# A hybrid decoder layer on one core: the mixer's queues rearranged

## The reference, cut to what matters

```
proj = xn @ w_in                      # one projection, 51 column tiles of 128
A: three groups (window, dilation) = (128,1), (512,4), (2048,16), 4 heads of 64:
   o_g = softmax(q k^T, banded) v ;  lse_g
   alpha = softmax over the groups of lse ;  o_a = sum_g alpha_g * o_g
B: gated delta rule, 4 heads of 128: conv + silu on q, k, v; L2 norms of q, k; chunks;
   per chunk (I + M) u = rhs, M strictly lower triangular; state carried on
   o_b = rms_norm(o_b) * silu(z)
y = sigmoid(gate_a) * (o_a @ w_pa) + sigmoid(gate_b) * (o_b @ w_pb) ;  out = y @ w_o
```

## Time and profile before

| | |
|---|---|
| three runs, median (range) | 1662.61 us (1659.88 to 1666.7) |
| the profiled execution | 1656.37 us |
| its span | 1654.6 us |
| mean granted clock of TensorE | 0.978 |
| PE, PEld busy | 94%, 77% |
| DVE, ACT, POOL busy | 59%, 41%, 52% |

### The profile page before, as it was taken

One profiled execution on the slowest core, in us unless ns is written; L12 is line 12 of the kernel. 1 busy time (PEld: TensorE's weight loads), 2 busy tenths in 40 slices (PEclk: granted clock), 3 DMA queues, 4 the chain that ended last, 5 costly groups with the idle time before them and its releaser, 6 DMA issues.

```text
span 1654.6 us, 21066 instructions
## 1 busy us (share of the span) xinstructions
PE 1554.6 (94%) x7625; PEld 1280.4 (77%) x7625; DVE 971.3 (59%) x1421; ACT 676.6 (41%) x1059; POOL 863.1 (52%) x675
## 2 busy tenths in 40 slices
PE   6998878989999998789999999999999999999998
PEld 4787657878888787668778877788888888888886
DVE  6743424556464657565355136865655666688876
ACT  5754322223434353443432133544444444454445
POOL 4567655655545443335733346988887778200011
PEclk9999989999999999899999999999999999999999
DMA  5132433334354444333437121333333333697685
GB/s 168 58 102 77 121 88 104 101 113 134 111 163 112 127 137 125 111 86 100 150 117 278 54 102 45 96 98 112 96 102 102 102 102 105 215 324 227 191 265 181
DMA packets 228147, 215.26 MB, mean 130 GB/s; under 512 B 25764, under 2 KB 176844, under 8 KB 228044
## 3 DMA queue, kind: packets, MB, share of 16 engines
q1 hardware_dynamic: 227824, 213.83, 41.9%
q10 hardware_dynamic: 220, 0.09, 0.0%
HBM read 156.85 MB, written 57.02 MB: 129 GB/s over the span
## 4 chain that ended last, share of the span: by engine, by line
PE 74%; DVE 10%; POOL 4%; DMA 4%; SPq 3%; ACT 3%; issue 2%; DVEq 0%; ACTq 0%; POOLq 0%
PE acc L1796 17%; PE acc L2852 12%; PE acc L2862 7%; PE bank_ab L2852 7%; PE att_ps L2852 5%; PE acc L672 5%; PE bank_ab L1745 5%; PE bank_ab L2862 3%; PE att_ps L2862 3%; PE acc L2221 3%; DMA m<-m_d 2%; DVE prod L1517 1%; PE bank_ab L2221 1%; PE att_ps L2221 1%; PE att_ps L1862 1%
## 5 line engine op out<-in xcount | busy, mean ns | idle before, releaser
L1241 POOL TENSOR_TENSOR w_low<-w_raw,w_high 128x512 fp32r<-128x512 f32 x96 | 126.1, 1314 | 173.0 <-ACT w_high L1335 172.7
L1796 PE MATMUL acc<-xh,w_high 128*128 128x512 f32 x384 | 160.4, 418 | 12.4 <-ACT m_one L1346 9.7
L1796 PE MATMUL acc<-xl,w_high 128*128 128x512 f32 x384 | 152.9, 398 | 0.0
L1796 PE MATMUL acc<-xh,w_low 128*128 128x512 f32 x384 | 152.7, 398 | 0.0
L1241 POOL TENSOR_TENSOR w_low<-m_sum,w_high 128x512 fp32r<-128x512 f32 x72 | 98.2, 1364 | 97.8 <-ACT w_high L1335 97.8
L1796 PE MATMUL acc<-m_t_high,w_high 128*128 128x512 f32 x288 | 120.5, 418 | 13.4 <-POOL w_low L1241 13.3
L1796 PE MATMUL acc<-m_t_high,w_low 128*128 128x512 f32 x288 | 114.7, 398 | 0.0
L1796 PE MATMUL acc<-m_t_low,w_high 128*128 128x512 f32 x288 | 114.5, 397 | 0.0
L2628 POOL TENSOR_TENSOR f_h<-f_h,f_fw 128x512 f32<-128x512 f32 x8 | 11.3, 1416 | 171.2 <-ACT f_junk L2551 171.2
L1796 PEld LDWEIGHTS acc<-xh,w_high 128*128 128x128 f32 x384 | 74.5, 194 | 28.5 <-issue 11.6
L1796 PEld LDWEIGHTS acc<-xh,w_low 128*128 128x128 f32 x384 | 73.8, 192 | 16.7
(11 more groups left out here) (438 smaller groups left out, 4540.2 us busy)
## 6 DMA issues: line engine op xcount, KB each, us to landing
w_raw<-in_w_in_dram SPq DMA_DIRECT2D x96, 256.0 KB, 3.3
f_raw<-glu_d SPq DMA_DIRECT2D x66, 256.0 KB, 3.1
f_raw<-in_w_down_dram SPq DMA_DIRECT2D x55, 256.0 KB, 4.2
w_raw<-in_w_up_dram SPq DMA_DIRECT2D x24, 512.0 KB, 5.2
glu_d<-u_free_high SPq DMA_DIRECT2D x22, 512.0 KB, 4.7
u_raw_even<-in_w_up_dram SPq DMA_DIRECT2D x20, 512.0 KB, 4.9
att_d<-staging SPq DMA_DIRECT2D x18, 512.0 KB, 3.4
f_raw<-gsum_d SPq DMA_DIRECT2D x33, 256.0 KB, 3.6
```

The costliest lines, as they stand in the source:

```text
L1241: g.tensor_tensor(vl[n % RING], source[it[2]], vh[n % RING].bitcast(F32), ALU.subtract).then_inc(s_vlo, 1)
L1796: mm = t_.matmul(to, w[:, k, :], xx[:, k, :], start=i < 4 and k == 0 and j == 0, stop=k == HK - 1 and j == 2, skip_group_check=True)
```

## The change

Eight edits, all in the order or the place of mixer work:

- `rnorm` becomes four items at (5,2), (5,3), (6,2), (6,3), each a power of 128x16; the tiny products of VectorE move to `rowsT`.
- `silu`, `gatesum` and `ssq` of the first convolution job move to later steps; the first split moves a step earlier.
- The delta rule starts 5 steps later (`DN_FROM`); its first solution stands further behind `kkD`; `T4` follows `P4` at once.
- The solution has four pieces: `sv0` for rows 2 to 4, `sv1` for rows 5 to 7, `sv2` and `sv3` for the two block products. `ts` moves behind the last.
- A new item `xb`: the product `XB` (L1638) goes from VectorE to GpSimd.
- The merging's three products and two sums go from VectorE to GpSimd; VectorE keeps the weights.
- For tiles 0 to 5 the two transposes of the merged tile stand in `a_pv` of the unit two later, in the other bank; their copy is ScalarE's there. For tiles 6 and 7 `cmbT` stays, later, with its copy on VectorE.
- The staged gates are stored raw (Copy); the sigmoid is taken in the merging stage, one activation a feature tile. The load of the row factors of the next chunk moves behind `ml`.

```diff
-        return [[(name, c)] for name in ("ml", "sv0", "sv1", "sv2", "ts", "tl", "ex")]
+        return [[(name, c)] for name in ("ml", "sv0", "sv1", "sv2", "sv3", "ts", "tl", "ex")]
...
+    out = [("load", 0)] + rest * 3 + [("xb", 0)] + kt + rest + kkD + rest * 3 + ml + rest * 2 + sv0 + rest + sv1 + rest
+    out += sv2 + rest + sv3 + rest
...
+        out += xb + [("vq", c)] + kt + [("P4", c), ("T4", c)] + kkD + rest + [("P5", c)] + ml + [("T5", c)] + ob + sv0
+        out += [("P6", c)] + sv1 + [("kS", c), ("T6", c)] + sv2 + [("vn", c)] + sv3 + ts + [("so", c)] + tl + ex
...
+RN = ((5, 2), (5, 3), (6, 2), (6, 3))
+CMB_LAST = {NT - 2: 20, NT - 1: 22}
-DN_FROM = 5 * TURN + 2 * HK
+DN_FROM = 5 * TURN + 3 * HK + 1
...
+                    part = rr[:].rearrange("p a h c -> p (a h c)")[:, j * n:(j + 1) * n]
+                    g.tensor_tensor(part, part, hp64[:, 0:n], ALU.pow).then_inc(s_rr, 1)
...
+                if kind == "cmb":
+                    i = it[1]
+                    X, cbs = cb, cbs2[i % 2]
+                    oc = ocb[:].rearrange("p (h c) -> p h c", h=AH)
+                    pool.wait_ge(s_co, 2 * i + 1)
+                    for q in range(NG):
+                        step(g.tensor_tensor(X[:, q, :, 0:DH], X[:, q, :, 0:DH],
+                                             cbs[:, 3, q].unsqueeze(2).to_broadcast([P, AH, DH]), ALU.mult))
+                    if i:
+                        pool.wait_ge(s_oast, 16 * i)
+                    step(g.tensor_tensor(oc, X[:, 0, :, 0:DH], X[:, 1, :, 0:DH], ALU.add))
+                    g.tensor_tensor(oc, oc, X[:, 2, :, 0:DH], ALU.add).then_inc(s_co, 1)
...
+                    if name == "xb":
+                        pool.wait_ge(s_rl, 16 * (c + 2))
+                        pool.wait_ge(s_ckqk[c % 2], 16 * (c // 2 + 1))
+                        if c:
+                            pool.wait_ge(s_a, a_taken[("kkD", c - 1)])
+                        g.tensor_tensor(XB[:], ckqk[c % 2][:, NH:2 * NH, :], spread[:, 1], ALU.mult).then_inc(s_dtm, 1)
...
-                            g.activation(stg[:], a[:], ACT.Sigmoid).then_inc(s_taken, 1)
+                            g.activation(stg[:], a[:], ACT.Copy).then_inc(s_taken, 1)
...
+                    act.wait_ge(s_atpe, att_no[it])
+                    if kind == "a_pv" and it[1] in merged_at:
+                        g.activation(ocb[:], att1[:, 2 * P:4 * P], ACT.Copy).then_inc(s_vk, 1)
...
+                    if it[1] in merged_at:
+                        pe.wait_ge(s_co, 2 * merged_at[it[1]] + 2)
+                        for j in range(2):
+                            last = t_.transpose(att1[:, (2 + j) * P:(3 + j) * P], ocb[:, j * P:(j + 1) * P], ident[:])
...
+                act.wait_ge(s_gate[(m + 1) % 2], 16 * ((m + 1) // 2))
+                nc.scalar.activation(gates[:, (m + 1) % 2], gates[:, (m + 1) % 2], ACT.Sigmoid).then_inc(s_gact, 1)
```

More of the change, by code:

```diff
@@ L118, in solving @@
     def solving(c):
-        return [[(name, c)] for name in ("ml", "sv0", "sv1", "sv2", "ts", "tl", "ex")]
+        return [[(name, c)] for name in ("ml", "sv0", "sv1", "sv2", "sv3", "ts", "tl", "ex")]
     rest = [("rest", None)]
-    ml, sv0, sv1, sv2, ts, tl, ex = solving(0)
+    ml, sv0, sv1, sv2, sv3, ts, tl, ex = solving(0)
     kt, kkD = front(0)
-    out = [("load", 0)] + rest * 3 + kt + rest + kkD + rest * 2 + ml + rest + sv0 + rest * 3 + sv1 + sv2 + rest
+    out = [("load", 0)] + rest * 3 + [("xb", 0)] + kt + rest + kkD + rest * 3 + ml + rest * 2 + sv0 + rest + sv1 + rest
+    out += sv2 + rest + sv3 + rest
     out += ts + rest + tl + rest * 2 + ex + rest
@@ L154, in mixer_schedule @@
                           1: [("split", 0, 0), ("sum", 0, 3), ("T", "low3")],
-                          2: [("T", "high1"), ("silu", 1)], 3: [("gatesum",), ("T", "low1")],
-                          4: [("split", 0, 1), ("sum", 0, 4)], 6: [("ssq", 0)]}.get(k, [])
+                          2: [("T", "high1")], 3: [("split", 0, 1), ("sum", 0, 4), ("T", "low1")],
+                          5: [("silu", 1)], 6: [("gatesum",)]}.get(k, [])
         items.append(("evac", n))
@@ L182, in mixer_schedule @@
                     items.append(("one", p))
+                    if p == 0:
+                        items.append(("ssq", 0))
                     if p == 0:
@@ L244, in mixer_schedule @@
                             c = u[1]
-                            for d, step in ((3, ("cload", c)), (9, ("cmbA", c)), (12, ("cmb", c)), (17, ("cmbT", c))):
+                            steps = [(3, ("cload", c)), (9, ("cmbA", c)), (12, ("cmb", c))]
+                            steps += [(CMB_LAST[c], ("cmbT", c))] if c in CMB_LAST else []
+                            for d, step in steps:
                                 at_slot.setdefault(slot + d, []).append(step)
@@ L710, in mixer @@
     unit_no = count(units)
+    merged_at = {(0, c + 2): c for c in range(NT) if c not in CMB_LAST}
+    v_done, oc_done, copies = {}, {}, 0
+    for u in units:
+        if u in merged_at:
+            copies += 1
+            oc_done[merged_at[u]] = copies
+        if unit_no[u] < len(units):
+            copies += 1
+            v_done[unit_no[u] + 1] = copies
     stores = [u for u in units for _ in range(2 if u[0] == 2 else 1)]
@@ L718, in mixer @@
         assert c == 0 or order[("cmb", c - 1)] < order[("cload", c)]
-        assert c == 0 or order[("cmbT", c - 1)] < order[("cmb", c)]
+        assert c not in oc_done or order[("cmb", c)] < order[("a_pv", (0, c + 2))] < order[("cmb", c + 1)]
     s_tri, s_const, s_masks, s_small = sem("m_gate_masks_ready"), sem("m_const_step"), sem("m_masks_ready"), sem("m_small_loaded")
@@ L1243, in x_gpsimd @@
                 if kind == "rnorm":
[L1244 to L1250, removed]
@@ L1507, in solve @@
             def solve(part, c):
-                if part == 0:
-                    dve.wait_ge(s_ml, 16 * (c + 1))
-                    if c:
-                        dve.wait_ge(s_ts, 16 * c)
-                    link(g.tensor_copy(strided(t_, BASE, [diag, 2], [1, 1]), strided(m_, 1, [diag, 2], [1, 1])))
-                    for i in range(2, half):
+                if part < 2:
+                    if part == 0:
+                        dve.wait_ge(s_ml, 16 * (c + 1))
+                        if c:
+                            dve.wait_ge(s_ts, 16 * c)
+                        link(g.tensor_copy(strided(t_, BASE, [diag, 2], [1, 1]), strided(m_, 1, [diag, 2], [1, 1])))
+                    for i in (range(2, half - 3), range(half - 3, half))[part]:
                         pr = strided(prod[0:NBLK * NH], 0, [i * i, 2], [i, i], [1, i])
@@ L1522, in solve @@
                 low = strided(t_, half * BASE, [BASE, half], [1, half])
-                if part == 1:
+                if part == 2:
                     link(g.tensor_tensor(pr, strided(m_, half, [1, half], [0, half], [BASE, half]),
```

81 lines of the change are left out of this document (41 added, 40 removed).

## The result

| | before | changed |
|---|---|---|
| median of four runs, one chip | 1661.24 us (1657.45 to 1666.7) | 1619.9 us (1616.26 to 1624.55) |
| ratio, 95% interval | | 0.975 [0.971, 0.979] |
| the profiled execution, its span | 1656.4, 1654.6 us | 1621.0, 1619.2 us |
| mean granted clock of TensorE | 0.978 | 0.992 |

The forecast was 1620 us. Between the profiled executions it promised 42.5 us, and 35.4 came.

A forecast was written before the change was run, and what follows sets the result against it. TensorE, busy 84 to 95% of the mixer, bounds the kernel; only gaps and slow-clock stretches can be won. Terms sum to -42.5 us, from 1656.4 to 1613.9 profiled; adding 6.2 gives a 1620 us median, own range 1602 to 1638.

The forecast's parts named there:

- Opening, -3: Product of squares, which waits 2.4 us for ScalarE, moves three k-steps later: -3 us, bounds -4 and +2.
- Later first loads, -3: Chunks' first loads go behind the weight room GpSimd's sum needs, easing w_low waits: -3 us, bounds -6 and +3.
- Powers in pieces, 0: GpSimd's row-norm power in four pieces: one w_low wait becomes two, about 4.4 and 5.1 us; net 0.
- all covered: Best bound of the powers term, -9.9 us: TensorE's whole wait for w_low there gone.
- First solution, -8.5: First solution 15 steps behind kkD, not 9: TensorE's 9.7 us wait goes, a 3.5 us cost appears; -8.5 us.
- Solution in pieces, -9 and -8: Half a solution's first part moves behind the copies of P6 and O: -9 us for P6, -8 for O.
- Merging, -25: Merging on GpSimd, transposes beside the values' product, raw gates: transposes wait for exponentials alone; -25 us, bounds -32 and -10.
- Spreading, +14: GpSimd waits for the solution's load at the spreading, delaying low parts of weights: +14 us, bounds 0 and +35.
- Sigmoid in the merging stage, 0: Six activations of 1.9 us while ScalarE is otherwise idle there: 0 us, bounds 0 and +6.
- New waits eat half: Rival, chance 0.17: GpSimd's added work passes waits on, spreading at its upper +35; about 1641 us.
- Slower: Rival, chance 0.07: SP issues the solution's load late, GpSimd stands 7 us longer in seven chunks; about 1680 us.
- It doesn't do what it says: Rival, chance 0.05: VectorE and the exponentials were the merging's real limit, not ScalarE's copy; 1655 us.

The follow-up runs named there:

- e1: Changed kernel with the powers of the row norms in one piece of 128x64 in place of four; 1619.5 us, 0.975 of before.
- e3: Changed kernel with the first part of a solution whole again, ahead of the copies of P6 and O; 1629.2 us, 0.982 of before.
- e4: Changed kernel with the first chunk's solution 9 steps behind its kk product again, in two neighbouring parts; 1622.7 us, 0.978 of before.
- e5: Changed kernel with the merging's three products and two sums back on VectorE; 1642.8 us, 0.989 of before.
- e7: Changed kernel with the merged tiles' transposes back in their old place and all their copies on ScalarE; 1627.2 us, 0.980 of before.
- e8: Changed kernel with merging on VectorE, sigmoid at the gates' evacuation, and transposes apart with ScalarE's copy; 1656.1 us, 0.9965 of before.
- e12: e11 with two GpSimd sums of 128x2048 cut into eight of 128x512 and the first chunk's matrix load three k-steps later; 1599.3 us, 0.962 of before.
- e11: Changed kernel with powers as ScalarE square root and VectorE reciprocal, and the spreading moved behind the next item; 1599.0 us, 0.964 of before.

## Why the prediction was right, point by point

*Opening, -3: right, and covered in the profile.* The wait for the product of squares is gone. In `e1` and `e3` the ninth copy starts at 157.5 us, 2.9 before that of the kernel before. In the changed kernel's own profile it starts at 161.9, since a later rise of the clock, and the collision of VectorE with GpSimd at 33 us that it led to, cost 4.4 us (last section). It is no part of the change that the prediction or the code names. Without it the profiled executions would stand some 39.8 us apart (35.4 + 4.4).

*Later first loads, -3: right.* Before, TensorE waited 1.55 us for the first chunk and 2.33 for `w_low` between 198 and 218 us; neither is there now, and the stretch won 4.6 us.

*Powers in pieces, 0: right for the pieces*, also in their split, 4.15 and 4.83 us for the predicted 4.4 and 5.1. The stretch lost 2.9 us all the same. `e1` loses as much, so it lies in what moved with them, the small products in front of the row factors' transposes (1.70 us), which the prediction left at nothing. The bound of -9.9 kept for "all covered" was to be had, 10.5 to 14.4 us by the three measures, but by other engines.

*First solution, -8.5.* The stretch won 13.7 us, with the gap of 9.7 gone and 16 matmuls moved out. The new place is 6 of it by the traces (`e4`), and by the end 0.4 to 4.1; another part is the order of SP's queue. The wait named next, for the weight rooms behind the stores of m, is there, 3.74 us at 237.26 where 2.2 was put.

*Solution in pieces, -9 and -8.* Measured as one edit 9.3 us (7.8 to 11.9 by the three measures). The first term is about its size. The second is not this edit's: O's wait went, but not by the pieces.

*Merging, -25: right cause, wrong weights.* Undone it costs 36.2 us, but that price is for a kernel with the other edits in it. Between the marks around it, the kernel before took 299.2 us and the changed one 286.0, so 13.2 were won there, where the forecast's -25 and most of its +14 met. Whether 25 was too small is not shown. The step gave the 6.35 us wait of one tile its right cause, ScalarE's copy, and named the chain mask, maximum, exponentials as the residue. Its weight was misjudged: the three products and two sums on VectorE were priced by the 3 us they take off that chain, and by themselves they are 22.9 us with the clock behind the waits (`e5`), while the transposes' new place is 7.3 (`e7`). The 2.19 us of the earlier trace rows for the three products came from one of three slow tiles: the other five took 1.10.

*Spreading, +14: oversized.* GpSimd waits 16.5 us for the load, as the step said it would, but TensorE's later waits for low parts are 8.4 us, and moving the spreading returned 4.6 of these. Steps in reserve took the rest.

*Sigmoid in the merging stage, 0: right.* From the last mark to the end it is 833.2 against 833.3 us, with six activations of 1.92 us more.

So the sum was near partly by luck, because its errors had both signs: the merging, as undone, worth more, the spreading costing less, the pieces, O above all, worth less, and the collision on top. The terms measured by undoing them (36.2 + 9.3 + 2.8 = 48.3 us) are 7 us above the 41.3 that came. The spreading may account for about 5 of it. The rest is not settled: `e8` shows that these prices hold only together with the other edits, so they need not add up.

*The rivals.* "New waits eat half" did not come, since the reserve in steps absorbed half of GpSimd's wait. "Slower" needed 6 us a chunk of a late load: from its store to the issue of its load it was 1.6 to 4.7 us, where before it went up to 11.4. SP's long waits did get shorter. "It doesn't do what it says" is excluded by its time, 1655 us, and by `e8`, but it was half right on the mechanism: the chain through VectorE to the exponentials weighs more (22.9 us) than the place of ScalarE's copy (7.3).

## What to carry to other kernels

When a wait ends with a copy, price what stands in the queue ahead of the producer too. A busy share of 59% did not make VectorE's work free: 2.3 us a tile ahead of the mask cost nearly 3 us a tile. Where an engine is slow at one function, moving it beats cutting it: four pieces of the power brought nothing, a square root and a reciprocal on two engines that had room brought some 12. An edit's worth depends on what stands beside it: without the new merging all the others brought 5.7 us. And a wait removed early in a list can turn up at the next blocking item of an in-order queue, so check what that queue reaches sooner.

## What the runs showed of the hardware

**VectorE waited out whole instructions of GpSimd.** In the norm stage GpSimd runs two sums of 128x2048, 4.6 us each. VectorE's scaling of 128x1024 comes beside them. GpSimd and VectorE before:

```profile
27.21 10.22 POOL L1221 TENSOR_TENSOR m_b_full<-xh,xl 128x2048 f32<-128x2048 f32 x2
...
31.69 1.28 DVE L587 SCALAR_TENSOR_TENSOR n_xn<-n_x,small,n_n1w 128x1024 f32<-128x1024 f32 x1
```

in the changed kernel:

```profile
27.38 9.09 POOL L1241 TENSOR_TENSOR m_b_full<-xh,xl 128x2048 f32<-128x2048 f32 x2
...
32.96 4.59 DVE L595 SCALAR_TENSOR_TENSOR n_xn<-n_x,small,n_n1w 128x1024 f32<-128x1024 f32 x1
```

and in `e12`, with eight short sums:

```profile
27.18 10.99 POOL L1242 TENSOR_TENSOR m_b_full<-xh,xl 128x512 f32<-128x512 f32 x8
...
32.65 1.87 DVE L595 SCALAR_TENSOR_TENSOR n_xn<-n_x,small,n_n1w 128x1024 f32<-128x1024 f32 x1
```

The 13 traces with the long sums fall into two sorts by when VectorE gets there, and the first sum ends between 31.5 and 32.0 us. In `e1` (31.23), `e3` (31.30) and before (31.69) it took 1.63, 1.48 and 1.28 us, and GpSimd's pair took 1.1 us longer. In the ten others it came between 31.60 and 32.96 and took 4.6 to 5.6 us, ending in all of them between 37.1 and 37.6, some 1.1 us after the pair was over. TensorE stood 3.2 to 4.2 us for it. Beside the short sums it stood 0.4. When VectorE gets there hangs on TensorE's transposes, which hang on the clock: it rose at 25.7 us in `e1` and about 29 us in the changed kernel (matmuls of 0.63 and then 0.39 us). So 4.4 us of an execution's time are decided by a difference of 0.3 us at 31 us (31.30 in `e3`, 31.60 in `e7`). It goes the other way too: in `e12` a `w_low` of GpSimd took 2.12 us in place of 1.29 while VectorE ran the first solution.

The Trainium skill, "SBUF — State Buffer", section "Who interferes with whom", calls the lock between this pair of engines exclusive; the traces agree. VectorE's difference with one input in PSUM (L603) took its 1.23 us beside the same sums.

**GpSimd's power is slow by the column.** 128x64 took 10.56 us and 128x16 2.91, where ScalarE's square root of 128x64 took 0.26 and VectorE's reciprocal 0.55. The four powers of the changed kernel:

```profile
L1268 POOL TENSOR_TENSOR rr<-rr,hp 128x16 f32<-128x16 f32 x4 | 11.6, 2909 | 0.7 <-DVE rr L1638 0.7
```

**A short wait can cost more than its length.** In `e12` a wait of 3.62 us gave back 6.5, since the clock behind it fell to the lower level; in `e11` and `e12` the same wait of 1.79 us stood once without and once with such a fall, and with it the step took 3.2 us more. Which of the two it is, the length of the wait alone does not tell.
